# Seven products for eight in the gate and up half of a feed-forward stage, with three weight sums made by adding transfers

## The reference

```python
def swiglu_ffn(x, w1, w3, w2):
    return (jax.nn.silu(x @ w1) * (x @ w3)) @ w2
...
        y = swiglu_ffn(x, w1[l], w3[l], w2[l])
        x = layer_norm_2(DEEPNORM_ALPHA_2 * x + y, ln_g[l, 2], ln_b[l, 2])
```

## Time and profile before

| what | value |
|---|---|
| median of 3 runs | 3269.99 us (3266.74 to 3270.38) |
| profiled execution, its own time | 3264.95 us |
| its span, first to last instruction | 3263.0 us |
| TensorE busy | 3227.7 us (99%) |
| VectorE busy | 2024.9 us (62%) |
| ScalarE busy | 1353.9 us (41%) |
| GpSimd busy | 0.2 us |
| mean granted TensorE clock | 0.997 of full |
| moved by DMA | 642.80 MB, mean 197 GB/s |

### The profile page before, as it was taken

One profiled execution on the slowest core, in us unless ns is written; L12 is line 12 of the kernel. 1 busy time (PEld: TensorE's weight loads), 2 busy tenths in 40 slices (PEclk: granted clock), 3 DMA queues, 4 the chain that ended last, 5 costly groups with the idle time before them and its releaser, 6 DMA issues.

```text
span 3263.0 us, 41319 instructions
## 1 busy us (share of the span) xinstructions
PE 3227.7 (99%) x17437; PEld 2781.7 (85%) x17437; DVE 2024.9 (62%) x1659; ACT 1353.9 (41%) x908; POOL 0.2 (0%) x4
## 2 busy tenths in 40 slices
PE   9999999999999999999999999999999999999998
PEld 8888888888888888888888888888888988888886
DVE  7566566667786666665465787764556544445556
ACT  4333555433344444443333443343333444444332
POOL 0000000000000000000000000000000000000000
PEclk9999999999999999999999999999999999999999
DMA  8645456677555555555655445654454655555553
GB/s 316 216 155 185 172 209 215 214 269 280 209 179 204 193 182 191 180 200 193 218 174 185 173 174 191 225 212 162 168 181 169 219 193 180 193 191 182 197 193 138
DMA packets 285000, 642.80 MB, mean 197 GB/s; under 512 B 11048, under 2 KB 16980, under 8 KB 273876
## 3 DMA queue, kind: packets, MB, share of 16 engines
q1 hardware_dynamic: 270000, 587.50, 52.4%
q10 hardware_dynamic: 14884, 53.59, 4.5%
HBM read 622.18 MB, written 18.87 MB: 196 GB/s over the span
## 4 chain that ended last, share of the span: by engine, by line
PE 95%; DVE 4%; DMA 1%; ACT 0%; issue 0%; SPq 0%; ACTq 0%; DVEq 0%
PE ps L1172 47%; PE ps L1051 43%; PE ps L1046 4%; PE ps L1176 1%; DVE wlo L1681 1%; DMA wraw<-in_w_in 0%; DVE tok L1917 0%; DVE tok L1922 0%; DVE tok L2607 0%; DVE tok L2606 0%; DMA s_b<-in_sg_ln_b 0%; DVE bst L1905 0%; DVE tok L1902 0%; DVE act_hl L1745 0%; DVE alt_hl L1745 0%
## 5 line engine op out<-in xcount | busy, mean ns | idle before, releaser
L1681 DVE TENSOR_TENSOR wlo<-wraw,whi 128x2048 fp32r<-128x2048 f32 x549 | 1244.8, 2279 | 682.6 <-ACT whi L630 674.1
L630 ACT ACTIVATE whi<-wraw 128x2048 fp32r<-128x2048 f32 x549 | 1042.5, 1906 | 1365.6 <-PE ps L1172 622.0
L1172 PE MATMUL ps<-act_hl,whi 128*128 128x512 f32 (+2 forms) x3936 | 915.1, 379 | 0.6 <-DVE m_k L1792 0.6
L1172 PEld LDWEIGHTS ps<-act_hl,whi 128*128 128x128 f32 (+1 forms) x3936 | 708.4, 188 | 126.4 <-DVE m_k L1792 0.7
L1051 PE MATMUL ps<-whi,act_hl 128*128 128x512 f32 x2128 | 661.9, 392 | 1.4 <-DVE wlo L1681 1.1
L1172 PE MATMUL ps<-act_hl,wlo 128*128 128x256 f32 x3696 | 503.6, 283 | 0.0
L1172 PEld LDWEIGHTS ps<-act_hl,wlo 128*128 128x128 f32 x3696 | 485.4, 191 | 17.3
L1051 PEld LDWEIGHTS ps<-whi,act_hl 128*128 128x128 f32 x2128 | 396.2, 188 | 84.2 <-issue 1.9
L1051 PE MATMUL ps<-wlo,act_hl 128*128 128x512 f32 x1064 | 414.4, 389 | 0.0
L1051 PE MATMUL ps<-whi,f_h 128*128 128x512 f32 x672 | 261.4, 389 | 0.0
L1051 PE MATMUL ps<-whi,f_l 128*128 128x512 f32 x672 | 261.4, 389 | 0.0
(11 more groups left out here) (324 smaller groups left out, 2053.1 us busy)
## 6 DMA issues: line engine op xcount, KB each, us to landing
wraw<-in_w SPq DMA_DIRECT2D x132, 1024.0 KB, 5.1
wraw<-in_w_in SPq DMA_DIRECT2D x118, 1024.0 KB, 5.3
wraw<-in_ffn_in SPq DMA_DIRECT2D x88, 1024.0 KB, 5.0
wraw<-laid_narrow_units SPq DMA_DIRECT2D x68, 1024.0 KB, 4.8
wraw<-in_ffn_out SPq DMA_DIRECT2D x44, 1024.0 KB, 5.0
wraw<-in_w_branch SPq DMA_DIRECT2D x16, 1024.0 KB, 5.0
wraw<-in_w_mix_out SPq DMA_DIRECT2D x16, 1024.0 KB, 7.5
wraw<-in_w_out SPq DMA_DIRECT2D x16, 1024.0 KB, 5.1
```

The lines of the kernel that those rows point to most:

```text
L630: act.activation(whi[:, slot, k, c], wraw[:, slot, k, c], ACT.Copy).then_inc(hi_done, 1)
L1172: return pe.matmul(o, left, right, start=start, stop=stop, skip_group_check=True)
L1681: dve.tensor_tensor(wlo[:, slot, k, c], wraw[:, slot, k, c], whi[:, slot, k, c].bitcast(F32), ALU.subtract).then_inc(lo_done, 1)
```

## The change

Only the gate and up half of this stage changes, from its second block on (10 of 11), and how hidden values reach the down products.

- **Seven products.** Let the tokens be two tiles (0 and 1) and the first two units of rows be 0 and 1. These make a 2 x 2 block product: four pieces of activations by four weight units (gate 0 and 1, up 0 and 1). It took eight products of one token tile by one unit; now it takes seven, with sums of activations (`mixes`, made once, four of them) and sums of weights (four per block). Rows 2 and 3 of the input are multiplied as before, for both tiles at once. A block is now 11 **parts** (`PARTS`) instead of 8 units: parts 1, 3, 4, 5, 7, 8 and 10 are for one product of 12 matmuls, parts 2, 6, 9 and 11 for two of 12.
- **The form** is that of the down products: tokens are held in TensorE, 512 weight columns stream past, and results have tokens on the partitions. Small sums on VectorE put the seven together (`first_t`, `v_t`, `w_t`, `fifth_t`).
- **Weight sums.** Three of the four are made by DMAs that add to what is in the tile, issued by GpSimd (`accum_op`): up 0 onto gate 0 in `part_a` (part 5), up 0 onto up 1 (part 8), up 1 onto `part_a` (part 7). VectorE makes the fourth: gate 1 onto `part_a` (part 10). SP loads seven units per block in place of eight.
- **Hidden values** are turned by eight 128 x 128 transposes on TensorE one block later (`turn_hidden`), copied out by ScalarE and sent to memory. The down products read them back piece by piece (`load_stage`).
- The list of each engine is written out for the ten blocks, where it was a loop.

```diff
-          ("ffn2_in", 8 * FB), ("ffn2_out", 4 * FB)]
+          ("ffn2_in", 8 + 11 * (FB - 1)), ("ffn2_out", 4 * FB)]
...
+PARTS = ["a", "k0", "d", "b", "a", "k1", "a", "d", "k0", "a", "k1"]
+def part(i, j):
+    return BASE["ffn2_in"] + 8 + 11 * (i - 1) + j
...
+            for i in range(1, FB):
+                ring = BASE["ffn2_in"]
+                sp.wait_ge(lo_done, part(i - 2, 10) if i > 2 else ring)
+                load_part(i, 1, gate, 0)
+                sp.wait_ge(lo_done, part(i - 1, 9) if i > 1 else ring + 5)
+                load_part(i, 2, gate, 2)
+                sp.wait_ge(lo_done, part(i - 1, 8) if i > 1 else ring + 6)
+                load_part(i, 3, up, 1)
+                if i > 1:
+                    sp.wait_ge(fourth_sum_made, i - 1)
+                else:
+                    sp.wait_ge(lo_done, ring + 7)
+                load_part(i, 4, gate, 1)
+                sp.wait_ge(lo_done, part(i - 1, 11) if i > 1 else ring + 8)
+                load_part(i, 6, up, 2)
+                sp.wait_ge(lo_done, part(i, 2))
+                load_part(i, 9, gate, 3)
+                sp.wait_ge(lo_done, part(i, 6))
+                load_part(i, 11, up, 3)
...
+            def hi_part(i, j):
+                g = w.at("unit")
+                assert g == part(i, j)
+                if PARTS[j - 1] == "a" and j > 1:
+                    if j == 5:
+                        act.wait_ge(first_sum_in, 16 * i)
+                    elif j == 7:
+                        act.wait_ge(third_sum_in, 16 * i)
+                    else:
+                        act.wait_ge(fourth_sum_made, i)
+                elif j == 8:
+                    act.wait_ge(second_sum_in, 16 * i)
+                else:
+                    act.wait_ge(part_in[part_name(i, j)], w.at(f"part {part_name(i, j)}", 16))
+                act.wait_ge(unit_done, g - SLOTS)
+                act.activation(whi[:, (g - 1) % SLOTS], part_raw(i, j), ACT.Copy).then_inc(hi_done, 1)
...
+                hi_part(i, 5)
+                if i == 1:
+                    act.wait_ge(block0_hidden, 1)
+                    send_hidden(0)
+                if i == FB - 1:
+                    act.wait_ge(lo_done, part(i - 1, 10))
+                    load_stage(0)
+                    load_stage(1)
+                act.activation(first_t[:, :], ps[:, 0:UNIT], ACT.Copy).then_inc(first_copied, 1)
+                hi_part(i, 6)
+                hi_part(i, 7)
+                hi_part(i, 8)
+                if i > 1:
+                    copy_turned(i - 1, (2, 4))
+                hi_part(i, 9)
+                act.activation(fifth_t[:, :], ps[:, 5 * UNIT:6 * UNIT], ACT.Copy).then_inc(fifth_copied, 1)
+                hi_part(i, 10)
+                hi_part(i, 11)
+                for n in range(4):
+                    hi_part(i + 1, n + 1) if i < FB - 1 else hi(1)
+                    if n == 2:
+                        act.wait_ge(gates_read, 2 * i)
+                        act.activation(gate_t[:, :, :], gate_t[:, :, :], ACT.Silu).then_inc(gates_mapped, 1)
+            for n in range(2, FB):
+                act.wait_ge(hidden_ready, FB + n - 1)
+                load_stage(n)
...
+            def part_products(x, banks, begin, end):
+                n = w.at("unit")
+                pe.wait_ge(lo_done, n)
+                slot = (n - 1) % SLOTS
+                for k in range(CB):
+                    for (h, l), bank in zip(x, banks):
+                        for j, (wt, op) in enumerate(((whi, h), (whi, l), (wlo, h))):
+                            ins = mm(ps[:, bank * UNIT:(bank + 1) * UNIT], op[:, k, :], wt[:, slot, k, :],
+                                     bank in begin and k + j == 0, bank in end and k == CB - 1 and j == 2)
+                ins.then_inc(unit_done, 1)
...
+                part_products([tokens_of(0, 0)], (0,), (0,), (0,))
+                if i > 1:
+                    pe.wait_ge(gates_read, 2 * (i - 1))
+                else:
+                    pe.wait_ge(silu_used, w.at("used"))
+                part_products(both(2 * CB), (1, 6), (1, 6), ())
+                if i > 1:
+                    pe.wait_ge(ups_read, 2 * (i - 1))
+                else:
+                    pe.wait_ge(mixes_ready, 1)
+                part_products([mixed_tokens(3)], (3,), (3,), ())
+                part_products([tokens_of(0, CB)], (1,), (), ())
+                if i > 1:
+                    turn_hidden(i - 1, (2, 4))
+                    pe.wait_ge(fifth_copied, i - 1)
+                part_products([mixed_tokens(2)], (5,), (5,), (5,))
+                part_products(both(2 * CB), (3, 7), (7,), ())
+                if i > 1:
+                    pe.wait_ge(turned_copied, 2 * (i - 1))
+                part_products([mixed_tokens(1)], (2,), (2,), (2,))
+                part_products([mixed_tokens(0)], (4,), (4,), (4,))
+                part_products(both(3 * CB), (1, 6), (), (1,))
+                part_products([tokens_of(1, CB)], (6,), (), (6,))
+                part_products(both(3 * CB), (3, 7), (), (3, 7))
...
+        @block.gpsimd
+        def _(pool):
+            for i in range(1, FB):
+                second = rows(a["w3_2"][0], 0, i * UNIT)
+                pool.wait_ge(lo_done, part(i, 1))
+                pool.dma_start(part_a[i % 2][:, :, :], second, accum_op=ALU.add).then_inc(first_sum_in, 16)
+                pool.wait_ge(lo_done, part(i, 3))
+                pool.dma_start(part_raw(i, 8), second, accum_op=ALU.add).then_inc(second_sum_in, 16)
+                pool.wait_ge(lo_done, part(i, 5))
+                pool.dma_start(part_a[i % 2][:, :, :], rows(a["w3_2"][0], UNIT, i * UNIT), accum_op=ALU.add).then_inc(third_sum_in, 16)
...
+                link(tt(mix_x[:, 0], x[1, 0], x[0, 0], ALU.subtract))
+                link(tt(mix_x[:, 1], x[1, CB], mix_x[:, 0], ALU.subtract))
+                link(tt(mix_x[:, 2], x[1, 0], x[1, CB], ALU.subtract))
+                tt(mix_x[:, 3], x[0, CB], mix_x[:, 1], ALU.subtract).then_inc(mixes_made, 1)
...
+                lo_part(i, 5)
+                lo_part(i, 6)
+                lo_part(i, 7)
+                dve.wait_ge(lo_done, part(i, 7))
+                tt(a_raw, a_raw, part_raw(i, 4), ALU.add).then_inc(fourth_sum_made, 1)
+                lo_part(i, 8)
+                lo_part(i, 9)
+                lo_part(i, 10)
+                dve.wait_ge(first_copied, i)
+                dve.wait_ge(unit_done, part(i, 7))
+                link(tt(v_t[:, :], bank_of(2), first_t[:, :], ALU.subtract))
+                lo_part(i, 11)
+                dve.wait_ge(unit_done, part(i, 8))
+                link(tt(w_t[:, :], bank_of(4), v_t[:, :], ALU.add))
+                dve.wait_ge(fifth_copied, i)
+                link(tt(v_t[:, :], v_t[:, :], fifth_t[:, :], ALU.add))
+                if last:
+                    split_piece(0)
+                    split_piece(1)
+                next_low(1)
+                dve.wait_ge(unit_done, part(i, 9))
+                tt(gate_t[:, 0, :], bank_of(1), first_t[:, :], ALU.add).then_inc(gates_read, 1)
+                next_low(2)
+                dve.wait_ge(unit_done, part(i, 10))
+                tt(gate_t[:, 1, :], bank_of(6), w_t[:, :], ALU.subtract).then_inc(gates_read, 1)
+                dve.wait_ge(gates_read, 2 * i)
+                link(tt(w_t[:, :], w_t[:, :], fifth_t[:, :], ALU.add))
+                next_low(3)
+                if i > 1:
+                    dve.wait_ge(hidden_turned, i - 1)
+                dve.wait_ge(unit_done, part(i, 11))
+                tt(up_t[:, 0, :], bank_of(3), v_t[:, :], ALU.add).then_inc(ups_read, 1)
+                tt(up_t[:, 1, :], bank_of(7), w_t[:, :], ALU.add).then_inc(ups_read, 1)
+                dve.wait_ge(ups_read, 2 * i)
+                dve.wait_ge(gates_mapped, i)
+                tt(up_t[:, :, :], up_t[:, :, :], gate_t[:, :, :], ALU.mult).then_inc(tokens_hidden, 1)
+                dve.wait_ge(tokens_hidden, i)
+                next_low(4)
```

More of the change, by code:

```diff
@@ L1426, in ffn @@
                 gate_up(True)
-                per = {"unit": 8, "conv": 1, "used": 1}
-                with pe.Fori(1, FB) as i, w.loop(i, 1, FB - 1, per):
-                    gate_up()
+                if by_tiles:
+                    for i in range(1, FB):
+                        seven_products(i)
+                else:
+                    per = {"unit": 8, "conv": 1, "used": 1}
+                    with pe.Fori(1, FB) as i, w.loop(i, 1, FB - 1, per):
+                        gate_up()
                 def piece(fresh, last, parity):
@@ L2590, in _ @@
+            for n in range(2, FB):
+                lo(4)
+                dve.wait_ge(unit_done, BASE["ffn2_out"] + 4 * (n - 1))
+                split_piece(n)
+            lo(4)
+            w.at("unit", UNITS - w.now("unit"))
             ahead[0] = 0
```

178 lines of the change are left out of this document (173 added, 5 removed).

## The result

| | before | after |
|---|---|---|
| median | 3266.9 us (3264.68 to 3270.38, 8 runs) | 3277.95 us (3275.58 to 3282.95, 8 runs) |
| span of the profiled execution | 3263.0 us | 3273.8 us |
| one block of the stage | 44.53 us | 45.25 us |

A forecast was written before the change was run, and what follows sets the result against it. TensorE was taken to bound the kernel. Blocks of 24.5 + 2 × 10.0 + 1.5 = 46.0 us against 44.53 gave +15 over ten, plus 2.7 and 1.0 once: +19 on 3270, 3289 us; 8-in-10 range 3246 to 3375.

The forecast's parts named there:

- Floor, 41.8 us: TensorE's work per new block: 180 matmuls at 0.2267 us plus 1.0 for turns, against 44.53 before.
- Cover of ScalarE and VectorE, nothing: Their work per block, 27.1 and 34.2 us, fits into 41.8 if nothing holds them up; cost nothing.
- SP's queue, nothing: Seven loads stay in order; the fourth waits for a sum made some 20 us before it is needed; cost nothing.
- The chain, 24.5 + 2L: Time between roundings of part 7, through first and third sums; above L of 8.6, each microsecond costs 2 per block.
- L = 10.0: Low part to landing of its adding transfer: 9.7 us for a pair of loads, for two reads, plus 0.34 issue.
- The second transfer, +1.5 us per block: On GpSimd's queue between first and third, it pushes the third back by some 1.5 us with L near 10.
- One-offs, +3.7: Once each: TensorE's wait at part 2 of the first new block, +2.7; last block's turns in first down piece, +1.0.
- Hidden values over memory, nothing: Hidden values go to memory and back, 0.5 MB each way, with a 21.8 us piece to arrive; cost nothing.
- TensorE waits at parts 7 and 8: Sign to look for: TensorE idle before parts 7 and 8, with a block period near 24.5 + 2L + 1.5.
- Sums in time: Faster rival: L under about 9.0 keeps blocks near the floor, -23 us, 3247 us; chance 0.36.
- Four times a load: Slower rival: adding takes DMA engines four times a load, L 14 or more, blocks 54 us, 3369 us; chance 0.14.
- Requests held up by VectorE: Rival: GpSimd's requests wait for VectorE, L grows by up to 2.29, blocks 50.6 us, 3335 us; chance 0.08.

The follow-up runs named there:

- no_sums: The changed kernel with all three adding transfers left out, GpSimd only raising the semaphores; median 3243.62 us, ratio 0.9933 to before, blocks of 41.71 us.
- all_moves: Changed kernel with loads as tiles free, third sum on VectorE, small operations behind low 1, copies earlier, last block's second split later; 3243.41 us, 0.9926 to before.
- plain_loads: The changed kernel with GpSimd's three adding transfers made plain loads to the same tile, sums not made; median 3241.67 us, ratio 0.9930 to before.

## Why the prediction was right, and where it was off

- **Floor, 41.8 us**: 41.71 measured. By the medians no_sums came out 22 us under before, 23 by the text. (One step inside it is off: the other form alone gives 44.53 − 8 × 5.44 = 1.0 us per block, so 10 us, where the text has 11. Nothing else uses it.)
- **Cover of ScalarE and VectorE, nothing**: right. Without sums neither holds TensorE up.
- **SP's queue, nothing**: wrong. The text checks the load behind the fourth sum, finds it 20 us early and puts the order of the seven loads at no cost. But the load of part 2 stood first and held back two others whose tiles were free. Sending them as tiles came free took 1.4 us off a block (45.25 to 43.89).
- **The chain, 24.5 + 2L**: right in form. With each transfer's own time, 24.5 + L1 + L3 gives 46.0 and 44.3 for blocks of 46.07 and 44.41, and the first issue at 20.05 for 20.3.
- **L = 10.0**: the value was near (first sum 9.8 to 12.2, median 11.0; third 8.9 to 11.7, median 9.3), the reason half of it. The two reads are real: 5.8 us of the engines against 3.0. The Trainium skill, Collectives: The Full Stack, section The bandwidth ceiling: the fold count and why AG ≠ RS ≠ AR, has it of reduce-scatter that the add needs two source reads and so halves the rate. This case agrees with that rule (1.95 times), for transfers of one core on GpSimd's queue. But I treated L as a price of the transfer. For the first sum it is the time until full engines have worked off SP's loads: issuing it 2.1 us earlier gained nothing, sending the loads 4.4 us earlier gained 12 us. The text had counted 41 us of the engines' work per block (0.86 × 45.25 = 39 measured) and called a queue "likelier", and then gave it no step of its own.
- **The second transfer, +1.5 us per block**: the term of the sum that failed. Left out, it changes no block (45.44 for 45.25). It made 46.0 of what would otherwise have been 44.5, and stood in, by luck, for the loads ahead of the first sum. Blocks measured 45.25: +0.7 each for +1.5.
- **One-offs, +3.7**: the wait at part 2 of the first block is 2.8 (2.7 forecast). Not in the sum: the clock at 0.50 behind it, and behind three later waits. Added up over stretches of 2 us from 2560 to 3040, the missing clock is 6.8 us in the change and 1.7 in no_sums. The text names this only among what would be seen. TensorE also waits 1.7 us for VectorE at the first down products, which the text does not have. The last block takes 50.96 us, 5.7 over the others, and 2.5 over them even without sums (44.20 for 41.71). The two hidden pieces that VectorE splits ahead of low 1 take 1.92 us each; how much of either excess is theirs is not shown, since with one of them moved, in all_moves, the last block is still 1.8 over.
- **Hidden values over memory, nothing**: right. In the down products TensorE waits for no read of them.
- **The total**: from the first new block's Silu to the last one's it is 412.9 us against 9 × 44.53 = 400.8, +12; the ends give back 1. Forecast +19.
- **TensorE waits at parts 7 and 8**: right places, but at part 7 it is for ScalarE's copies, not low 7, which the text had not listed among what is queued behind the late rounding.
- **Rivals.** Sums in time: this is what plain_loads and all_moves do, with medians of 3242 and 3243 (3247 in the text). Four times a load: out, 1.95 measured. Requests held up by VectorE: out. GpSimd's issues took 1.28 to 1.30 us in 29 of 30 cases and 1.43 in the first. Two of them, at 2564.61 and 2575.38, had VectorE idle beside them and took 1.29 and 1.28 us, no less than those that a low part ran beside. The Trainium skill, SBUF — State Buffer, section Who interferes with whom, has a VectorE instruction with two inputs in SBUF contend with GpSimd's reads and not with its writes; the trace agrees.

## What to carry to other kernels

A transfer's time to landing belongs to the whole set of transfers in flight: before pricing it as a latency, list what the other queues have sent ahead of it, and look at the DMA share in stretches of a few microseconds rather than over a block. Where the engines are idle and then full, order the loads by when their tiles come free. A limit that hides behind another shows only once that one is lifted, so a move that gains nothing alone is tried again later.
